# Running a decoder layer's delta rule between the pieces of its prompt attention

## The reference

```python
p = h @ w_in                                   # q, k, v, forget logits | conv q, k, v, alpha, beta, z | gates
# forgetting attention of the prompt, causal, blocks of 128 queries, 8 heads
s = q @ k.T / 8 + cq[:, None] - ck[None, :]    # c: running sum of log forget values
o_a = softmax(where(causal, s, -inf)) @ v
# attention of the samples: 32 pages of 128 cached keys and values each, for 8 samples
# delta rule of the prompt, 4 heads, 8 chunks of 64 tokens; gc: running sum of g in a chunk
lower = (k * beta) @ k.T * decay               # decay = exp(gc_i - gc_j), lower triangle of a chunk
u, w  = solve(I + lower, [v * beta, k * beta * exp(gc)])
attn  = (q @ k.T) * decay
for each chunk:                                # the scan over the state S, 128 x 128 per head
    v_new = u - w @ S
    o = (q * exp(gc)) @ S + attn @ v_new
    S = S * exp(g_last) + (k * exp(g_last - gc)).T @ v_new
o_g = rmsnorm(o) * silu(z)
y = (sigmoid(gate_a) * (o_a @ w_a) + sigmoid(gate_b) * (o_g @ w_g)) @ w_out
```

## Time and profile before

| | us |
|---|---|
| median of three runs (lowest, highest) | 1748.49 (1741.89, 1749.19) |
| the profiled execution, its own time | 1743.63 |
| its span | 1741.4 |
| attention loop, from its first score product (844.12) to 1007.16 | 163.0 |
| tail for samples 4 to 7, to 1012.50 | 5.3 |
| delta rule, to the end of its last product at 1181.60 | 169.1 |
| TensorE busy in the span | 1601.5 (92%) |
| mean granted clock of TensorE, of full speed | 0.952 |

### The profile page before, as it was taken

One profiled execution on the slowest core, in us unless ns is written; L12 is line 12 of the kernel. 1 busy time (PEld: TensorE's weight loads), 2 busy tenths in 40 slices (PEclk: granted clock), 3 DMA queues, 4 the chain that ended last, 5 costly groups with the idle time before them and its releaser, 6 DMA issues. The chain is left out here.

```text
span 1741.4 us, 31220 instructions
## 1 busy us (share of the span) xinstructions
PE 1601.5 (92%) x12682; PEld 1430.2 (82%) x12682; DVE 605.8 (35%) x893; ACT 501.0 (29%) x742; POOL 132.6 (8%) x152
## 2 busy tenths in 40 slices
PE   5999998998888999999899968987997999998996
PEld 4999998998777888778554448976987999998995
DVE  3333332211635562234232244323516333332113
ACT  4222222222422462221223322204335222222222
POOL 0000000000450002231100002202000000000000
PEclk9999999999899999999899978977998999999998
DMA  3222222221569979999999910002411222222221
GB/s 102 96 89 92 95 86 91 88 95 42 189 193 389 310 256 362 324 338 383 336 325 319 370 68 1 1 1 92 146 61 50 95 87 94 94 87 85 98 83 49
DMA packets 111786, 268.24 MB, mean 154 GB/s; under 512 B 15373, under 2 KB 15886, under 8 KB 110938
## 3 DMA queue, kind: packets, MB, share of 16 engines
q1 hardware_dynamic: 105370, 241.88, 40.2%
q0 software_dynamic: 6336, 25.21, 4.0%
HBM read 252.78 MB, written 14.26 MB: 153 GB/s over the span
## 5 line engine op out<-in xcount | busy, mean ns | idle before, releaser
L130 DVE TENSOR_TENSOR w_low<-w_raw,w_high 128x1024 fp32r<-128x1024 f32 (+1 forms) x180 | 232.9, 1296 | 764.2 <-ACT w_high L126 753.0
L126 ACT ACTIVATE w_high<-w_raw 128x1024 fp32r<-128x1024 f32 (+1 forms) x180 | 200.6, 1116 | 754.8 <-PE psum L151 715.4
L147 PE MATMUL psum<-h_high,w_high 128*128 128x260 f32 x1408 | 286.0, 284 | 16.5 <-DVE h_low L227 16.5
L151 PE MATMUL psum<-h_high,w_low 128*128 128x260 f32 x1408 | 284.7, 284 | 0.0
L149 PE MATMUL psum<-h_low,w_high 128*128 128x260 f32 x1408 | 284.5, 284 | 0.0
L147 PEld LDWEIGHTS psum<-h_high,w_high 128*128 128x128 f32 x1408 | 218.0, 189 | 19.0 <-issue 14.4
L151 PEld LDWEIGHTS psum<-h_high,w_low 128*128 128x128 f32 x1408 | 218.2, 189 | 0.0
L149 PEld LDWEIGHTS psum<-h_low,w_high 128*128 128x128 f32 x1408 | 217.6, 189 | 0.0
L147 PE MATMUL psum<-a_high,w_high 128*128 128x260 f32 x704 | 146.4, 289 | 10.4 <-DVE a_low L383 10.4
L147 PE MATMUL psum<-mix_h_high,w_high 128*128 128x260 f32 x704 | 148.0, 292 | 6.7 <-DVE mix_h_low L227 5.8
L149 PE MATMUL psum<-mix_h_low,w_high 128*128 128x260 f32 x704 | 143.1, 285 | 0.3 <-issue 0.3
(11 more groups left out here) (301 smaller groups left out, 1844.7 us busy)
## 6 DMA issues: line engine op xcount, KB each, us to landing
kv_ring<-in_cache_k SPq DMA_DIRECT2D x256, 256.0 KB
kv_ring<-in_cache_v SPq DMA_DIRECT2D x256, 256.0 KB
w_raw<-in_w_gu SPq DMA_DIRECT2D x88, 512.0 KB
w_raw<-in_w_dn SPq DMA_DIRECT2D x32, 704.0 KB
w_raw<-in_w_proj SPq DMA_DIRECT2D x44, 512.0 KB
spill<-h_f POOLq DMA_DIRECT2D x20, 260.0 KB
gates<-spill POOLq DMA_DIRECT2D x16, 260.0 KB, 3.5
w_raw<-in_w_merge SPq DMA_DIRECT2D x8, 512.0 KB
```

Source lines behind the costliest of these rows:

```text
L126: act.activation(w_high[:, u, 0:nk, :], w_raw[:, u, 0:nk, :], ACT.Copy).then_inc(high_done, 1)
L130: dve.tensor_tensor(w_low[:, u, 0:nk, :], w_raw[:, u, 0:nk, :], w_high[:, u, 0:nk, :].bitcast(F32), ALU.subtract).then_inc(low_done, 1)
L147: pe.matmul(out[h], w_high[:, u, k, :], high[:, k0 + j, tok[h]], start=s, stop=False)
L151: mm = pe.matmul(out[h], w_low[:, u, k, :], high[:, k0 + j, tok[h]], start=False, stop=e)
```

## The change

The delta rule's block is gone. Its work is a list of 57 **steps**: spread, raw and turn for each of four heads, four for the inverse's start, 21 level steps, four solves and 16 for the scan. The attention loop of each engine calls step 2t in its first half and step 2t + 1 in its second, so that the last step runs in iteration 28 of 34.

- A level step does the first product of level and head i, and the two products (inverse and its transpose) of i - 1. The last level no longer updates the inverse that is not transposed.
- PSUM: steps use banks 5, 6 and 7. Scores and transposed probabilities of a tile share bank t mod 2 (before: own bank 2 for the transposes), so `scores(t)` waits for the copy of t - 2 in place of its exp. Attention's output moves to bank 2, the samples' (r = 1) turns to bank 3 and values to bank 4, with one bank where there were two.
- SBUF: the tiles of steps lie over x, the weight buffers, the spill buffers and the projection's slots. So SyncE loads the first two merge blocks, z, and stores the state behind the last value pages, and x comes back only in the gated norm's block. ScalarE waits for the samples' stored states, the level masks and all spilled blocks before the first exp.
- The negated g (four small products, one pass of VectorE) goes ahead of the transposes of v.
- The samples' tail uses a second copy of the head mask, that GpSimd loads between masks of levels.

The core of the diff (the steps' bodies on VectorE are the passes named above, with other banks):

```diff
-            attention(proj, rows, cum, h_high, h_low, fox_o, onew, parts, x_back)
-            gdn(proj, cum, gdn_o, onew, parts)
+            core(proj, rows, cum, h_high, h_low, fox_o, onew, zt, z_in)
+            gated(proj, gdn_o, zt, z_in, x_back)
             merge(fox_o, gdn_o, x_back)
...
+            steps = [(kind, h) for h in range(GH) for kind in ("spread", "raw", "turn")]
+            steps += [("inverse", h) for h in range(GH)]
+            steps += [("level", i) for i in range(HL + 1)]
+            steps += [("solve", h) for h in range(GH)]
+            steps += [(kind, n) for n in range(NCH) for kind in ("state", "update")]
+            def step_at(t, half):
+                n = 2 * t + half
+                return steps[n] if n < len(steps) else None
...
+                    n_merge = n0 + NB
+                    sp.wait_ge(w_act, 2 * GH)
+                    for m in range(2):
+                        load_block(sp, a["w_merge"], m, n_merge + m, m, KD)
+                    sp.dma_start(zt[:, :, :], a["spill"][0:GH, :, :].rearrange("h p t -> p h t")).then_inc(z_in, 16)
...
+                    act.wait_ge(s_stored, 32)
+                    act.activation(ident_r[:, :], ident[:, :], ACT.Copy)
+                    act.wait_ge(levels_in, 32)
+                    act.activation(mask_r[:, :], mask[:, :], ACT.Copy).then_inc(parts_high, 1)
+                    for u in range(2):
+                        act.wait_ge(spilled[u], 16 * (NB - Z0) // 2)
...
                     for t in range(N + 2):
                         if t < N:
                             exp(t)
+                        if step_at(t, 0):
+                            gdn_step(*step_at(t, 0))
                         if 1 <= t <= N:
                             turned(t - 1)
-                        if t % 8 == 1 and t > 8:
-                            out(t // 8 - 1)
...
                         if t >= 2:
-                            pe.wait_ge(f_exp, t - 1)
+                            pe.wait_ge(ft_copy, t - 1)
                         bank = psum[:, t % 2, :]
...
-                            mm = pe.transpose(psum[:, 2, j * P:(j + 1) * P], prb[:, t % 2, j * P:(j + 1) * P],
+                            mm = pe.transpose(psum[:, t % 2, j * P:(j + 1) * P], prb[:, t % 2, j * P:(j + 1) * P],
...
+                        elif kind == "level":
+                            if i < HL:
+                                h = i % GH
+                                pe.wait_ge(l_mask, i + 1)
+                                pe.wait_ge(l_act, GH + i)
+                                if i >= GH:
+                                    pe.wait_ge(l_upd, GH + 2 * (i - GH) + 2)
+                                for p in range(NQ):
+                                    mm = pe.matmul(pr(psum[:, 5, :], p), pr(lo_[i % 2][:, :], p), pr(dm[:, h, :], p),
+                                                   start=True, stop=True)
+                                mm.then_inc(l_pe, 1)
+                            if i:
+                                n, h = i - 1, (i - 1) % GH
+                                pe.wait_ge(l_act, GH + n + 1)
+                                if n:
+                                    pe.wait_ge(l_upd, GH + min(2 * n, n + HL - GH))
+                                if n < HL - GH:
+                                    for p in range(NQ):
+                                        pe.matmul(pr(psum[:, 6, :], p), pr(e_t[:, h, :], p), pr(tmp[:, h, :], p),
+                                                  start=True, stop=True)
...
                     for t in range(N + 2):
                         if t < N:
                             scores(t)
+                        if step_at(t, 0):
+                            gdn_step(*step_at(t, 0))
                         if t in key_at:
                             key_pair(1, key_at[t])
...
                         if t in value_at:
                             value_pair(1, value_at[t])
+                        if step_at(t, 1):
+                            gdn_step(*step_at(t, 1))
                         if t >= 2:
                             values(t - 2)
```

More of the change, by code:

```diff
@@ L568, in attention @@
             g_new = sem("states_updated")
+            levels_in = sem("level_masks_loaded")
+            parts_high = sem("high_parts")
+            parts_low = sem("low_parts")
+            p_bc = sem("prep_products")
+            p_act = sem("prep_scalar")
+            p_dve = sem("prep_vector")
+            p_raw = sem("prep_pairs")
+            p_last = sem("prep_last")
+            p_neg = sem("prep_negated")
+            p_turn = sem("prep_turned")
+            p_tok = sem("prep_token_major")
+            l_mask = sem("level_masked")
+            l_pe = sem("level_products")
+            l_act = sem("level_copied")
+            l_upd = sem("level_updated")
+            w_pe = sem("solved_products")
+            w_act = sem("solved_copied")
+            c_pe = sem("scan_products")
+            c_dve = sem("scan_steps")
+            c_out = sem("scan_out")
+            c_copy = sem("scan_out_copied")
+            g_store = sem("prompt_state_stored")
+            o_new = sem("gdn_new_placed")
             spill = h_f
@@ L624, in slot_of, with pr, pairs, over_pairs @@
                     return n if n < 4 else CV0 + 1 + n - 4 if n < 16 else K0 + n - 16
+                def pr(t, p):
+                    return t[:, p * P:(p + 1) * P]
+                def pairs(t):
+                    return t.rearrange("p (n k) -> p n k", n=NQ)
+                def over_pairs(t):
+                    return t.rearrange("p (o k) -> p o k", o=1).broadcast_to([P, NQ, P])
                 def by_head(t):
@@ L1258, in _ @@
                             peak(t)
-                        if t % 8 == 1 and t > 8:
-                            low(t // 8 - 1)
+                        if step_at(t, 0):
+                            gdn_step(*step_at(t, 0))
                         if t in take_at:
@@ L1265, in _ @@
                             values_spread(1)
+                        if step_at(t, 1):
+                            gdn_step(*step_at(t, 1))
+                        if t % 8 == 1 and t > 8:
+                            low(t // 8 - 1)
                     probs_sum(1)
@@ L1846, in gdn @@
+                o = proj[:, CV0:CV0 + GH, :]
                 z_dve = sem("gated_steps")
```

627 lines of the change are left out of this document (280 added, 347 removed).

## The result

The changed kernel took 1696.81 us (median of four runs, 1691.72 to 1699.92), the kernel before 1745.19 (four runs, 1739.95 to 1749.19) on the same chip. The ratio is 0.972, 95% interval 0.968 to 0.976. Two later sets of runs gave 1693.47 (ratio 0.969) and 1691.34 (0.967). So the change takes 48 to 57 us off, where 61 were forecast against the first median: 1687 was some 4 to 10 us too low, inside the range of 1670 to 1714.

What follows compares the result with a forecast made beforehand. TensorE bounds both stages, with the cache stream in attention and engine handoffs at low clock in the delta rule. New stages 279.2 against 337.5 us, 58.3 less, give 1685.3; plus 2 is 1687, range 1670 to 1714.

Steps and rivals of the forecast that it cites:

- The signs it named: What the new profile should show: iteration 6 about 60 us after first scores, DMA share about 0.55, exp(0) by 850.
- iterations 6 to 33: Attention loop after the preparation: 120.9 us of attention, 90.2 of steps, 2 of handoffs, at granted clock 0.97 or more.
- rival D: Clock stays at its lower level through iterations 6 to 28: at 0.60, +126 us, 1813; chance 0.05.
- Rival C: Handoffs show all along, each of 45 steps leaving 0.5 us open: +20, with clock dips about 1709; chance 0.10.
- what still waits in iterations 0 to 5: Preparation steps between attention pieces: handoffs not fully hidden leave TensorE waiting 8.2 us, bounds 0 and 33.
- clock in iterations 0 to 5: Preparation steps between attention pieces: a granted clock of 0.90 adds 5 us to 46.7 of work.
- rival B: Preparation keeps the clock at 0.64: 46.7 us of work take 73.0 instead of 59.9, total 1700; chance 0.12.
- the start's 0.9: Before the first scores: four small products and a negation ahead of the transposes cost 0.9 us, 0 to 1.8.
- The 2 added for the spread of runs: Whole kernel: 2 us added to 1685.3 because the timed runs' median lay 4.9 above the profiled execution.
- Costs given as nothing: Merge blocks, z and state issued behind the last value pages, and x's return in the gated part: 0 us.
- GpSimd beside VectorE: Iterations 7 to 17: up to 10 scalings wait 1.25 us each for GpSimd's masking, 12.5 in all, 1700; chance 0.03.

Runs made afterwards that it cites:

- the version with the start's products: Changed kernel plus ten unread 128x128x512 products in TensorE's idle time just before the first scores; 1688.73 us, ratio 0.968.

## Why the prediction was right, and where it was off

**The signs it named.** Held: iteration 6 came 63.9 us after the first scores (some 60), the DMA share fell to 0.56, ScalarE's copy for a spread was TensorE's longest wait up to the tail, exp(0) ran at 846.77, and no scaling took 1 us. Not held: iterations 6 to 33 took 222 us at 0.95 (213 at 0.97 or more), one page wait was 1.2 (none over 1), and the middle of the scan had 0.79, under the 0.85 that was to show rival D. The time was in the range although the clock was not as forecast.

**Handoffs and waits: right.** All waits for pages went but one of 1.2 us. The levels ran as priced: a group of four starts 0.89 after the last in the levels' rows,

```profile
938.01 1.06 PE L1763 MATMUL psum<-inverse,level_part 128*128 128x128 f32 x8
938.90 1.06 PE L1774 MATMUL psum<-gdn_tmp,inverse_t 128*128 128x128 f32 x8
939.79 1.06 PE L1777 MATMUL psum<-inverse_t,gdn_tmp 128*128 128x128 f32 x8
```

and the stretch of the levels has 0.5 us idle in 95.6. Rival C (0.5 left open at each step) is what the experiment with adjacent steps made, not the change. The tail took 5.4 (5.3 forecast). ScalarE's copy ahead of a spread is the longest wait of the preparation, as named:

```profile
893.16 0.49 PE L1723 MATMUL psum<-g_beta_high,sel_part 4*128 4x512 f32 x1 [1.68 <-ACT proj L995]
...
899.48 1.91 PE L1736 MATMUL psum<-gdn_tmp,proj 128*128 128x128 f32 x8
...
905.33 1.04 PE L1744 MATMUL psum<-ident,gdn_tmp 128*128 128x128 f32 x8
```

**Term "what still waits in iterations 0 to 5": too large.** 8.2 was forecast, 3.2 measured (0.32, 0.65, 0.16, 0.39 and 1.68). The low clock itself helped: slower products around a handoff cover more of it. In the version with the start's products iterations 3 and 4 ran at 1.00, and TensorE waited 0.64 and 0.57 there for VectorE where the changed kernel had no wait and 0.16.

**Term "clock in iterations 0 to 5": too small.** 5 was taken, from the nearer of two stretches (0.90). Measured: 60.71 busy less the 46.7 of work at full speed, 14.0, at a clock of 0.76. The rows above show it: after the wait of 1.68 eight records last 1.91 on L1736 that last 1.06 at the upper level. I tied the clock to the share of idle time. With 5% idle it was still 0.76, so that tie was the step that failed. The nearer row for such work was the preparation's own, 0.64, and 0.76 lies about halfway between that and 0.90: rival B's mechanism was at work at half its size. The two terms missed in opposite directions (5.0 too much, 9.0 too little), which is luck in the sum. Together they gave 63.9 us up to iteration 6, where 59.9 was forecast and 73.0 for rival B.

**Iterations 6 to 33: the clock of the scan was missing.** 222.2 were measured, 213.1 forecast (120.9 of attention, 90.2 of steps, 2 of handoffs). Idle were 0.34 in the levels and 1.20 for a page, so the 2 was enough; 213.1 - 2 + 1.5 + 10.4 of low clock in the scan is 223.0, against 222.2. I had given this only as rival D, for the whole of the loop at 0.60 and against it "the waits left there are some tenths". The waits are not what it takes: it came with no idle time at all, in iterations with the scan's products (23, 24 and 27). Rival D in small, in 20.7 us in place of 189. Two readings behind that rival were loose, without weight in the sum: the wait of 1.21 stood in every second chunk (four in eight, 4.9 us), not in each, and the stretch of 0.60 ran 18 us past the scan's last product; the scan alone, from 1132.67 to 1181.60, had 0.67.

**The sum.** From the first scores to the last sample product 291.5 were measured (843.40 to 1129.56 and 5.4 of tail), 278.3 forecast without the start's 0.9: 13.2 too few, 4.0 of them before iteration 6 and 9.1 behind it. The first scores came 0.7 earlier (843.40 for 844.12) instead of 0.9 later. The small products themselves cost what was priced: from the last key pair of the projection to the first scores it is 7.46 us (from 835.94), 6.48 before (from 837.64), 0.98 more. But the projection's end came 1.7 earlier, which no term of the sum has; the first scores lie anywhere from 843.18 to 845.81 in the profiles of all versions. So 1.7 of the measured gain has no cause in the forecast, nor is the 1.1 behind the first merge product (541.5 before, 540.4 after, both to the span's end). The net is 48.0 less in the profiles, not 58.3. The 2 added for the spread of runs was not borne out: the median lay 1.2 above the profiled execution in the first set, 5.1 and 1.2 below it in the two later ones.

**Costs given as nothing: right.** DMA share was 0.52 in the levels (0.55 forecast for the loop), and x, z and the state took 8.4, 9.1 and 9.0 from issue to landing, with no wait of TensorE for them:

```profile
x<-x_spill SPq DMA_DIRECT2D x1, 2080.0 KB, 8.4
...
silu_z<-spill SPq DMA_DIRECT2D x1, 1040.0 KB, 9.1
```

The masks held ScalarE up by 4.1 once, beside TensorE's work; TensorE shows no wait behind it.

**GpSimd beside VectorE: the mechanism exists, its price was hidden.** GpSimd's masking met VectorE's four copies of the sample group's new values once. GpSimd's row and VectorE's, of after, and VectorE's of before:

```profile
962.27 1.27 POOL L836 TENSOR_TENSOR level_part<-lower_t,levels 128x512 f32<-128x512 f32 x1 [1.84 <-PE psum L1763]
...
962.41 1.61 DVE L1153 COPY value_bc<-proj 128x128 f32<-128x128 f32 x4
```
```profile
913.39 0.62 DVE L1033 COPY value_bc<-proj 128x128 f32<-128x128 f32 x4
```

1.61 against 0.62; with GpSimd kept busy 3.3. The masking ended at 963.54, 1.13 us after the four copies had begun and 0.48 before they ended, so they look held until it was over. The Trainium skill, "SBUF — State Buffer", section "SBUF: two separate sides", says that a VectorE operation in a two-port mode and a GpSimd operation lock each other out for a whole instruction. Before the change no row had both at once; the runs now agree with it: copies and scalings are held up, and passes that read PSUM are not.

It cost TensorE nothing, as forecast: a scaling has some 4 us before it is asked for, and TensorE never waited for one in the levels.

## What to carry to other kernels

Laying a chain of dependent steps between the pieces of another stage pays by the handoffs it hides, and for that consecutive steps must stand apart: with the two steps of an iteration side by side, 41 of 53 us were gone. Price such a merged stage at the granted clock that its parts show, not at the share of idle time it will have: here the preparation and the scan kept a part of their low clock when the gaps were filled. And before tuning a few us of clock, time the same kernel several times; here its stage alone varied by 7 us.

## What the runs showed of the hardware

- TensorE's granted clock fell to its lower level with no idle time before it, among attention's pieces and the scan's products (1055.7 to 1105: 49.30 of 49.30 us busy, 0.79). The same iterations without the scan's products ran at 1.00. Neither large unread products (0.82 in iteration 23) nor a value pair in each iteration (0.84 in iteration 27) kept every iteration at 1.00.
- In the preparation the clock was 0.74 to 0.76 at 5% idle, 0.78 with large unread products before each spread, and 0.73 with half of the 4-row products replaced.
- VectorE's four copies from SBUF to SBUF took 2.6 times as long while GpSimd worked on SBUF (1.61 for 0.62), and its passes over PSUM as long as ever (0.687 and 0.688).
